# Loading expert weights as 16 KB a partition: down weights as one run, column pairs in the gate and up products, whole transfers in the middle rounds

## What is computed

```python
# n_tok = 256, d = 1024, w_gate, w_up: (32, 1024, 512), w_down: (32, 512, 1024)
weights, experts = ...            # 2 experts a token, from two routers
def run_block(args):
    tok, e = args
    xb = xf[tok]
    hid = jax.nn.silu(xb @ w_gate[e]) * (xb @ w_up[e])
    return hid @ w_down[e]
y = zeros.at[buf_t].add(outs * buf_w[:, None])
x = x + gt2 * y
return rms_norm(x, g_final)
```

## Time and profile before

| | |
|---|---|
| median of 3 runs | 946.2 us (943.51 to 946.67) |
| the profiled execution | 941.32 us |
| its span, from the first to the last instruction | 939.6 us |
| TensorE matmuls busy | 786.0 us, 84% |
| VectorE, ScalarE busy | 471.9 us, 338.1 us |
| mean rate of the DMA engines over the span | 297 GB/s |
| mean granted clock of TensorE | 0.941 |

### The profile page before, as it was taken

One profiled execution on the slowest core, in us unless ns is written; L12 is line 12 of the kernel. 1 busy time (PEld: TensorE's weight loads), 2 busy tenths in 40 slices (PEclk: granted clock), 3 DMA queues, 4 the chain that ended last, 5 costly groups with the idle time before them and its releaser, 6 DMA issues.

```text
span 939.6 us, 20123 instructions
## 1 busy us (share of the span) xinstructions
PE 786.0 (84%) x7481; PEld 600.4 (64%) x7482; DVE 471.9 (50%) x818; ACT 338.1 (36%) x509; POOL 54.8 (6%) x145
## 2 busy tenths in 40 slices
PE   8999999899999999999999997975575566776554
PEld 7999789678888887979989754543232333343222
DVE  4664787757786853776895633341221212232123
ACT  7443666453543436655873411211010101010112
POOL 4000000000000000020130000000000000000000
PEclk9999999999999999999999998998887979898797
DMA  7876332648989745562447979999999999999995
GB/s 236 290 277 220 111 107 75 224 147 317 342 298 333 264 151 205 160 216 91 136 152 284 424 270 420 420 422 421 422 423 421 423 420 422 423 421 423 421 423 214
DMA packets 97523, 278.78 MB, mean 297 GB/s; under 512 B 9375, under 2 KB 69194, under 8 KB 80074
## 3 DMA queue, kind: packets, MB, share of 16 engines
q1 hardware_dynamic: 97194, 277.95, 77.2%
q10 hardware_dynamic: 288, 0.27, 0.1%
HBM read 277.15 MB, written 1.05 MB: 296 GB/s over the span
## 4 chain that ended last, share of the span: by engine, by line
PE 57%; DMA 14%; SPq 12%; DVE 8%; ACT 5%; issue 4%; DVEq 0%; ACTq 0%; POOL 0%; POOLq 0%
SPq L861 10%; PE bank L2170 8%; DMA Whi<-in_w_up 6%; PE bank L385 5%; PE bank L387 5%; PE bank L386 5%; PE bank L2192 4%; PE bank L1808 4%; PE bank L1810 4%; PE bank L1809 4%; DMA projR<-in_w_up 3%; DMA Wlo<-in_w_up 3%; DMA Wlo<-in_w_gate_up 2%; DVE Whi_r L327 1%; PE acc L1834 1%
## 5 line engine op out<-in xcount | busy, mean ns | idle before, releaser
L385 PE MATMUL bank<-R_r,Whi_r 128*128 128x256 f32 x448 | 128.9, 288 | 3.0 <-DVE Whi_r L2233 2.6
L386 PE MATMUL bank<-R_r,Whi_r 128*128 128x256 f32 x448 | 126.9, 283 | 0.0
L3023 DVE TENSOR_TENSOR V<-V,bank 64x256 f32<-64x256 f32 x34 | 14.4, 424 | 216.0 <-ACT V L1530 216.0
L387 PE MATMUL bank<-R_r,Whi_r 128*128 128x256 f32 x368 | 104.3, 283 | 0.0
L385 PEld LDWEIGHTS bank<-R_r,Whi_r 128*128 128x128 f32 x448 | 86.0, 192 | 6.4 <-DVE Whi_r L2233 3.2
L1530 ACT ACTIVATE V<-bank 64x256 f32<-64x256 f32 x34 | 12.8, 375 | 204.7 <-PE bank L2170 204.7
L386 PEld LDWEIGHTS bank<-R_r,Whi_r 128*128 128x128 f32 x448 | 86.0, 192 | 0.1
L2170 PE MATMUL bank<-Whi,S 128*32 128x256 f32 x832 | 59.4, 450 | 30.9 <-DMA Whi<-in_w_up 30.6
L318 ACT ACTIVATE Whi_r<-Wlo 128x1024 fp32r<-128x1024 f32 x62 | 62.1, 1051 | 56.2 <-PE bank L387 53.7
L2170 PE MATMUL bank<-w_gate,S 128*32 128x256 f32 x352 | 52.2, 461 | 33.9 <-DMA projR<-in_w_up 33.9
L327 DVE TENSOR_TENSOR Whi_r<-Wlo,Whi_r 128x1024 fp32r<-128x1024 f32 x48 | 58.0, 1250 | 31.6 <-ACT Whi_r L318 31.6
(11 more groups left out here) (520 smaller groups left out, 1601.3 us busy)
## 6 DMA issues: line engine op xcount, KB each, us to landing
Wlo<-in_w_down SPq DMA_DIRECT2D x29, 1024.0 KB, 20.4
Wlo<-in_w_in SPq DMA_DIRECT2D x24, 1024.0 KB, 5.3
Wlo<-in_w_gate_up SPq DMA_DIRECT2D x22, 1024.0 KB, 7.7
Whi<-in_w_down SPq DMA_DIRECT2D x20, 1024.0 KB, 25.3
R<-in_w_down SPq DMA_DIRECT2D x18, 1024.0 KB, 25.4
Wlo<-in_w_ada SPq DMA_DIRECT2D x14, 1024.0 KB, 9.1
Whi<-in_w_gate SPq DMA_DIRECT2D x10, 1280.0 KB, 24.2
Whi<-in_w_up SPq DMA_DIRECT2D x10, 1280.0 KB, 26.9
```

The lines of the kernel that those rows point to most:

```text
L385: pe.matmul(o, w_hi[:, c], tile(x_hi, k), start=start, stop=False, skip_group_check=True)
L386: pe.matmul(o, w_hi[:, c], tile(x_lo, k), start=False, stop=False, skip_group_check=True)
L387: return pe.matmul(o, w_lo[:, c], tile(x_hi, k), start=False, stop=(k == KT - 1), skip_group_check=True)
```

## The change

The down weights of an expert are put on the partitions as four rows in one run of 16 KB: partition p holds rows 4p to 4p + 3. Hidden unit 4p + f must then stand on partition p, so the gate and up products of a band read the columns 4m + 2h, 4m + 2h + 1 for m = 0 to 127, with h = 0 or 1: pairs of columns in steps of four, in place of 256 neighbours. What they write lies as before, and the transposes are as before.

The loops over the rounds stand three times, for SyncE and for TensorE. In rounds 0 and 1 (`part` 0) the pieces and waits are as before, though a down piece is now half of each partition's 16 KB. In rounds 2 to 7 (`part` 1) gate, up and down are each loaded whole, 2 MB and 16 KB a partition; SyncE waits for `gu_done` ahead of gate and up, and TensorE for all of gate and up ahead of the first product. In rounds 8 and on (`part` 2) gate is loaded whole, up in its two pieces, and down in its two; TensorE waits for gate, makes 8 products of `ones` that nobody reads, then waits for the first piece of up, and before k = 5 for the second. (Two semaphores more, `fin_rinv` and `y_ready`, are put among the shared ones; their steps are the same.)

```diff
+        WHOLE = (2, 8)
...
-            def expert_part(name, e, par, halves=(0, 1)):
+            def expert_part(name, e, par, piece, full):
...
+                if name == "wd":
+                    rows, n = w.rearrange("a (p f) n -> p a (f n)", p=P), 1
+                    if piece is not None:
+                        c = slice(piece * 2 * D, (piece + 1) * 2 * D)
+                        rows, place = rows[:, :, c], place[:, c]
+                else:
+                    rows, n = w.rearrange("a (p k) n -> p a (k n)", p=P), 1
+                    if piece is not None:
+                        c = slice(piece * 5 * DE, (5, KT)[piece] * DE)
+                        rows, place = rows[:, :, c], place[:, c]
+                sp.dma_start(place.rearrange("p (a n) -> p a n", a=n), rows
+                             ).then_inc(sem(f"{full}_full{par}"), 16)
...
-                    for h in range(2):
-                        sp.wait_ge(*upto("gu_done" if h else "gu_half", used))
-                        expert_part("wg", number, par, (h,))
-                        expert_part("wu", number, par, (h,))
+                    if part == 0:
+                        for h in range(2):
+                            sp.wait_ge(*upto("gu_done" if h else "gu_half", used))
+                            expert_pieces("wg", number, par, (h,))
+                            expert_pieces("wu", number, par, (h,))
+                    else:
+                        sp.wait_ge(*upto("gu_done", used))
+                        expert_part("wg", number, par, None, "gu0")
+                        if part == 1:
+                            expert_part("wu", number, par, None, "gu1")
+                        else:
+                            expert_part("wu", number, par, 0, "gu1")
+                            expert_part("wu", number, par, 1, "gu2")
                     sp.wait_ge(*upto("yw_done", used))
-                    expert_part("wd", number, par)
+                    if part == 1:
+                        expert_part("wd", number, par, None, "wd0")
+                    else:
+                        expert_pieces("wd", number, par)
...
-            with sp.Fori(1, NO // NBUF) as i:
-                expert(i, 0)
+            with sp.Fori(1, WHOLE[0]) as i:
+                expert(i, 0, 0)
+            with sp.Fori(*WHOLE) as i:
+                expert(i, 0, 1)
+            with sp.Fori(WHOLE[1], NO // NBUF) as i:
+                expert(i, 0, 2)
...
                         if w is None:
-                            pe.wait_ge(*upto(f"gu_full{par}_0", i * 32 + 32))
+                            pe.wait_ge(*gu_full(0))
+                            if part == 2:
+                                for _ in range(8):
+                                    pe.matmul(bank[2][:, T:2 * T], ones[:, 0:P], ones[:, :],
+                                              start=True, stop=True)
+                            if part:
+                                pe.wait_ge(*gu_full(1))
                             pe.wait_ge(*upto("xw", before * 2 + 1))
...
-                                if w is None:
-                                    pe.wait_ge(*upto(f"gu_full{par}_1", i * 32 + 32))
+                                if w is None and part != 1:
+                                    pe.wait_ge(*gu_full(2 if part else 1))
                             for g in range(4):
-                                c = k * DE + (g % 2) * 256
-                                mm = pe.matmul(gu_bank(w)[g * WIN:(g + 1) * WIN, 0:256],
-                                               xw[:, k * WIN:(k + 1) * WIN],
-                                               (gate, up)[g // 2][:, c:c + 256],
+                                columns = (gate, up)[g // 2][:, k * DE:(k + 1) * DE].rearrange(
+                                    "p (m h c) -> p m h c", h=2, c=2)[:, :, g % 2, :]
+                                mm = pe.matmul(gu_bank(w)[g * WIN:(g + 1) * WIN, 0:256].rearrange(
+                                                   "p (m c) -> p m c", c=2),
+                                               xw[:, k * WIN:(k + 1) * WIN], columns,
                                                start=(k == 0), stop=(k == KT - 1))
...
-                            if f % 2 == 0:
-                                pe.wait_ge(*upto(f"wd_full{par}_{f // 2}", i * 16 + 16))
+                            if f == 0 or f == 2 and part != 1:
+                                pe.wait_ge(*wd_full(f // 2))
```

More of the change, by code:

```diff
@@ L863, in _, with expert_pieces @@
+            def expert_pieces(name, e, par, pieces=(0, 1)):
+                for h in pieces:
+                    expert_part(name, e, par, h, ("wd", "gu")[name != "wd"] + str(h))
             for j in range(2):
                 sp.wait_ge(*upto(f"proj2_done{j}", IN2_FULL // 512))
[L865 to L866 removed]
+            expert_pieces("wg", 0, 0)
+            expert_pieces("wg", 1, 1)
             sp.wait_ge(*upto("mix2_ready", 3))
[L868 removed]
+            expert_pieces("wu", 2, 2)
@@ L2209, in expert @@
                     if par < NBUF - 1:
-                        expert(i, par + 1)
-            with pe.Fori(0, NO // NBUF) as i:
-                expert(i, 0)
+                        expert(i, par + 1, part)
+            with pe.Fori(0, WHOLE[0]) as i:
+                expert(i, 0, 0)
+            with pe.Fori(*WHOLE) as i:
+                expert(i, 0, 1)
+            with pe.Fori(WHOLE[1], NO // NBUF) as i:
+                expert(i, 0, 2)
             total = pe.snap(pe_seen, min_val=1, max_val=MAXWIN)
```

41 lines of the change are left out of this document (19 added, 22 removed).

## The result

The changed kernel took **947.65 us** (median of 10, 946.15 to 949.81) against 944.28 us (median of 10, 941.92 to 946.67) for the kernel before on the same chip: the ratio is 1.0034, interval [1.0023, 1.0046], or 3.2 us slower. The forecast was 2.7 us faster. (Its 943.5 us went from a median of 946.2 us in three runs; from the 944.28 us measured beside the change, 2.7 us less would be 941.6.) The profiled execution took 947.48 us, with a span of 945.7.

What follows compares the result with a forecast made beforehand. The prediction took the expert stage to be bound by the transfers of the experts' weights; -4.0 us from transfers and +1.3 in the tail gave -2.7 us, a median of 943.5 us, range 939.6 to 947.6.

Steps and rivals of the forecast that it cites:

- The bound and the transfers: Expert stage bound by weight transfers; 16 KB packets take 612 ns, an expert 14.71 us instead of 14.92; -4.0 us together.
- Rival C: Packets of 16 KB bring little or nothing: 0 to -1.5 us from transfers, +1.3 in the tail, 946.0 to 947.5; chance 0.14.
- Column pairs at nothing: Gate and up products reading column pairs in steps of four cost nothing, bounds 0 and 71% of a pass.
- share x: Share by which column pairs lengthen each gate and up pass; the sum turns positive at 0.21, far bound 0.71.
- rival D: Slower: pairs lengthen passes; first issue 9.4x us later, last expert's end 3.7x; about 958 us at the far bound; chance 0.13.
- Whole transfers make waits coarser: Rounds 2 to 7: SyncE and TensorE wait longer for whole loads; cost nothing, up to 1.4 us once without slack.
- The tail: Round 9, last expert: -0.5 us if its clock is full, +1.3 us if half at first; +1.3 taken.
- rival B: The tail is warm, unread products end by the landing: -4.0 - 0.5, 941.7 us; chance 0.22.
- T: Moment at which the last weight piece releases a wait in round 9, put at 927.36 us before the change.
- Code: Fetching TensorE's three loop copies falls in rounds 2 and 8, where TensorE is behind or idle; nothing, at most 1 us.
- rival E: Other stalls, as of code in the tail; chance 0.06.

Runs made afterwards that it cites:

- m0: The changed kernel's transfers, piece order and column pairs, but one TensorE loop and no unread products; 0.9979 of the kernel before.
- e3: The kernel before with only down weights as one 16 KB run and column pairs, old loop and pieces; 1.0013 of the kernel before.
- h: The kernel before with whole transfers in rounds 2 to 8, one TensorE loop, old layout, no pairs; 0.9962 of the kernel before.
- m8: The changed kernel's transfers, order, pairs and eight unread products (rounds 8 and 9), but one TensorE loop; 0.9983 of the kernel before.
- e1: The changed kernel without the eight unread products, three loop copies kept; 0.9987 of the kernel before, repeated at 0.9991.
- u4: The changed kernel with four unread products instead of eight ahead of each expert of rounds 8 and 9; 0.9989 of the kernel before.

## Why the prediction was wrong, point by point

**The bound and the transfers: right.** Forecast: 615 ns a packet of 16 KB, 428 GB/s, 14.71 us an expert, -4.0 us. Measured: 614 to 615 ns by the packet records, 428 GB/s, 14.69 us. (By the wall clock give a fixed part of 7.1 ns, 44.9 less 37.8, where I wrote 7.5; it changes the sum by under 0.2 us.) For what the change moves whole, m0 has 373.5 us from first issue to last packet; 377.0 before and 0.9 for the pairs make it -4.4 us. Rival C falls.

**Column pairs at nothing: the step failed, small.** The share x of rival D is 0.05. Its rule, 9.4x before the first issue and 3.7x at the end, gives 0.65 us; measured were +1.1 us in the stretch. The first part is right, 9.4 x 0.05 = 0.5 us. The second did not come, the tail is no longer than before. What the rule lacked is 0.9 us up to the last packet, most of it where the queue nearly runs dry at expert 5 (counted from 0: 15.6 us for its bytes instead of 15.0, in e3 as in the changed kernel; 338 and 350 GB/s at 588 to 592 us in e3). That the longer passes of the first experts, which all stand in front of the release of a buffer there, add up to it is my reading; no run tests it alone.

**Whole transfers make waits coarser, at nothing: right.** The changed kernel's issues of round 2 take 0.33 to 0.38 us each, and the engines stay busy. The rate does sag at the change of mode, to 362 to 383 GB/s from 590 to 596 us, but e3 sags without a whole transfer, and h, with them and without pairs, takes 15.1 us for expert 5 where the kernel before takes 15.0: that is the pairs.

**The tail: +1.3 us was wrong both ways.** Between -0.5 (warm) and +1.3 (cold) I took the cold one. The kernel that this sum describes, with the unread products and without fetches, is m8: its tail is 0.3 us over the kernel before (mean of its two traces, 1.9), and its last pass is warm, as in rival B, behind 3.38 us of idleness. I had chosen by the length of the idle time, and that does not order them: in m8 itself 2.59 us ended cold (the eight took 5.40 us, expert 25), 3.38 warm. m0, cold and without the products, is 1.1 us over. The eight products take 3.71 us, not 3.4; my own row gives 3.7 (2.76 x 8 / 6), the 3.4 was a slip. T was 0.5 us late (the last packet ended at 926.83 us), which the differences do not feel. In the changed kernel the tail is +2.9 us in the first trace, +4.0 on average over three, for the reason that follows.

**Code, "nothing, at most 1 us": this is the step that turned the sign.** I looked where the fetches fall and found TensorE behind or idle, and did not ask what they do to a TensorE that the same change loads with 3.7 us more in just that round. Summed over one expert: unread 3.7 to 4.6, pass 3.85, idle 0.95, transposes and combine 1.25 (2.0 where the stall cuts the combine), stall 2.2 to 2.6, down 2.7 to 3.64 behind the stall (1.93 warm), together 14.7 to 17.5 less the overlaps; from pass to pass the trace has 15.6, 15.9 and 17.3 us against 14.9 of transfers. I took the unread products as a bridge over idle time, one at a time, at the last expert only. Measured instead of nothing: the fetches alone 1.7 us (e1 against m0), and with the unread products behind them another 2.6 us in the stretch, 4.2 by the times. Of rival E, which named code in the tail with 0.06, this is the case.

**Without the fetches the forecast would have looked right, in part by luck.** m8 has a stretch 2.4 us shorter than the kernel before (1.6 us by the times); I had said 2.7. But the pairs cost 1.4 us that I had put at nothing, and the tail was 1.0 us and the transfers 0.4 us better than I had them.

**The account of the changed kernel**, in the stretch: transfers -4.4, pairs +1.4 (0.5 + 0.9), fetches +1.7 (e1 against m0: 1.4 up to the last packet, 0.3 in the tail), order of pieces and cold pass +1.1 (m0's tail), unread products with fetches +2.6. Sum +2.4, measured +2.5; each term is the difference of two kernels in a chain from the one before to the changed one, so that they add up is no test of them. By the times +3.1. What is left of it outside this account, and the 1.6 us above, I can't place.

## What to carry to other kernels

Sum an engine's whole round, stalls and cold clock included, for every stage in which work is put into its idle time; idle time that two edits both count on is spent twice. Filler products belong where the real work can't start yet: with alternating pieces they took the place of 5/8 of the pass. And a special case is cheaper in the small loop of the engine that only issues (SyncE, adding the counts itself) than as another copy of TensorE's loop, where two copies were 11 more fetches of 16 KB.

## What was not expected of the hardware

- A fetch of 16 KB of instructions holds a DMA engine for 1.06 us, but where TensorE stands for it, it stands for 2 to 3 us in most cases (1.3 to 3.3 over all traces with copies). Behind the last stall the granted clock is 0.50 (rows above), which costs another 1.7 us at 32 down products; not behind each: in u4 it is 1.00 behind 1.75 us and 0.50 behind 2.99.
- A moving operand of 256 columns in steps of two, or in pairs in steps of four, makes a pass of 64 products 5% longer (3.84 and 3.85 us against 3.66), the same for both.
- The unedited first 540 us vary by 5.8 us between traces (537.3 to 543.1 us), far more than the transfer-bound stretch behind them (0.2 us in three pairs of traces).
